# A chain of two transformer-like blocks on one core: six modulation products moved into the even attention's loop, and eight smaller reorderings

## What is computed

```python
def first_block(x, p, w_in, ...):
    h = rmsnorm(x, g_pre);  proj = h @ w_in
    (qa, ka, va, gate_a, qi, ki, wi, qb, kb, vb, fb, gate_b) = split(proj)
    att_a = dsa_branch(qa, ka, va, qi, ki, wi)     # top-k keys by an indexer
    att_b = fox_branch(qb, kb, vb, log_f)          # causal, with forgetting
    m_a, m_b = split(sigmoid(h @ w_merge))
    out = (m_a * (att_a * silu(gate_a)) @ w_branch_a
         + m_b * (att_b * silu(gate_b)) @ w_branch_b) @ w_out
    x = x + rmsnorm(out, g_post)
    return x + rmsnorm(sigmoid(x @ w_ple_gate) * (p @ w_ple), g_ple)
# second block, 2 layers, on x and a context of 256 tokens; each layer l:
#   modulation = silu(c) @ w_mod[l]  -> 6 rows of 1024: shift, scale, gate
#   even layer: differential attention (8 heads x 2 maps) and a short convolution
#   odd layer: neighbourhood attention and a Fourier mix
```

## Time and profile before

| | us |
|---|---|
| median of three runs | 1328.12 (1324.62 to 1328.36) |
| the profiled execution | 1323.46 |
| its span | 1321.5 |
| PE busy | 1246.7 (94%) |
| DVE, ACT, POOL busy | 669.7, 630.4, 456.8 |
| granted clock of TensorE, mean | 0.985 |

### The profile page before, as it was taken

How to read it: one execution, slowest core, us unless ns; L and a number is a source line. 1 busy time by engine, 2 the same in 40 slices (tenths; PEclk the granted TensorE clock), 3 DMA queues, 4 the chain that set the end, 5 groups by cost and what they waited for, 6 DMA issues and landing times.

```text
span 1321.5 us, 19566 instructions
## 1 busy us (share of the span) xinstructions
PE 1246.7 (94%) x7148; PEld 993.4 (75%) x7148; DVE 669.7 (51%) x1296; ACT 630.4 (48%) x1351; POOL 456.8 (35%) x360
## 2 busy tenths in 40 slices
PE   7999999999999699679999999999999999999998
PEld 6877776776787477578887887887868878777776
DVE  4666965755315142454838668642624701555343
ACT  7544326654523244482346666644446422655533
POOL 5543443321344333260233333331451133222341
PEclk9999999999999899899999999999999999999999
DMA  6321541111431625332141220001243142222452
GB/s 230 132 72 64 192 159 64 61 37 44 156 137 66 252 103 185 128 104 104 52 151 69 105 105 33 33 33 64 96 177 142 65 149 74 68 93 64 160 156 67
DMA packets 28429, 140.33 MB, mean 106 GB/s; under 512 B 4304, under 2 KB 5712, under 8 KB 15728
## 3 DMA queue, kind: packets, MB, share of 16 engines
q1 hardware_dynamic: 21584, 117.72, 25.3%
q10 hardware_dynamic: 6752, 21.35, 4.9%
HBM read 122.74 MB, written 6.29 MB: 98 GB/s over the span
## 4 chain that ended last, share of the span: by engine, by line
PE 70%; DVE 11%; ACT 8%; POOL 4%; DMA 4%; issue 3%; ACTq 0%; DVEq 0%; SPq 0%; POOLq 0%
PE psum L648 42%; PE psum L676 5%; PE psum L768 4%; DMA w_raw<-stream 3%; POOL w_low L1231 2%; PE psum L811 2%; DVE arena L2298 2%; PE psum L1048 2%; DVE small L2295 2%; PE psum L1216 2%; PE psum L903 2%; ACT w_high L1407 2%; PE psum L636 2%; PE psum L889 1%; PE psum L1032 1%
## 5 line engine op out<-in xcount | busy, mean ns | idle before, releaser
L1231 POOL TENSOR_TENSOR w_low<-w_raw,w_high 128x512 fp32r<-128x512 f32 x256 | 345.2, 1362 | 683.5 <-ACT w_high L1407 683.3
L1407 ACT CAST w_high<-w_raw 128x512 fp32r<-128x512 f32 x256 | 153.6, 622 | 296.5 <-PE psum L648 176.1
L648 PE MATMUL psum<-x_high,w_high 128*128 128x512 f32 x528 | 219.4, 416 | 6.6 <-POOL w_low L1231 2.4
L648 PE MATMUL psum<-x_high,w_low 128*128 128x512 f32 x528 | 207.4, 393 | 0.0
L648 PE MATMUL psum<-x_low,w_high 128*128 128x512 f32 x528 | 206.8, 392 | 0.0
L648 PEld LDWEIGHTS psum<-x_high,w_high 128*128 128x128 f32 x528 | 99.9, 189 | 37.1 <-issue 15.8
L648 PEld LDWEIGHTS psum<-x_high,w_low 128*128 128x128 f32 x528 | 99.4, 188 | 21.8
L648 PEld LDWEIGHTS psum<-x_low,w_high 128*128 128x128 f32 x528 | 99.9, 189 | 16.5 <-issue 0.7
L648 PE MATMUL psum<-w_high,x_high 128*128 128x512 f32 x224 | 89.5, 400 | 3.0 <-ACT w_high L1407 2.2
L648 PE MATMUL psum<-w_high,x_low 128*128 128x512 f32 x224 | 88.0, 393 | 0.0
L648 PE MATMUL psum<-w_low,x_high 128*128 128x512 f32 x224 | 87.8, 392 | 0.0
(11 more groups left out here) (480 smaller groups left out, 2810.8 us busy)
## 6 DMA issues: line engine op xcount, KB each, us to landing
w_raw<-stream SPq DMA_DIRECT2D x98, 1024.0 KB, 4.8
x_kept<-arena ACTq DMA_DIRECT2D x8, 512.0 KB, 4.6
arena<-x_kept ACTq DMA_DIRECT2D x8, 512.0 KB, 6.3
arena<-bias ACTq DMA_DIRECT2D x8, 512.0 KB, 3.7
q_masked<-e_q_high SPq DMA_DIRECT2D x24, 96.0 KB, 2.5
arena<-x SPq DMA_DIRECT2D x4, 512.0 KB, 5.2
arena<-x ACTq DMA_DIRECT2D x4, 512.0 KB, 6.2
arena<-ctx ACTq DMA_DIRECT2D x4, 512.0 KB, 5.0
```

The costliest lines, as they stand in the source:

```text
L648: mm = pe.matmul(o, l, r, start=(first and n == 0 and kind != "fc"), stop=(last and n == len(passes) - 1))
L1231: pool.tensor_tensor(PLACE[u][1], RAW[:, g % 2, u % 4, :], PLACE[u][0].bitcast(F32), ALU.subtract).then_inc(w_lo, 1)
L1407: act.copy(PLACE[u][0], RAW[:, g % 2, u % 4, :]).then_inc(w_hi, 1)
```

## The change

Six of the twelve products, (0,4), (0,5), (1,0), (1,1), (1,2) and (1,3), leave the hosts mb1, wo0, wo1, pg0, pg1 and eo0. Each is done in whole (`modulate_whole`) at the end of step 2, 10, 18, 26, 34 and 42 of the even loop in bank 5, and its turn (`turn_row`) two steps later where i is below 4. In the stream each of the six granules of the slim chunks is followed by two product granules. ACT copies rows and columns in the next step, DVE adds the bias once behind e_ga. Casts in the loop go by `even_units`. Beside this: PE's waits for the copies of vb and n_v come later; prep_i(0) earlier on ACT and DVE; the index loop casts two steps later; two casts of n_k and those of oo0[4..7] are placed among other work; e_ga has its two first units ahead of the gate rows, with other banks from there to n_v. The diff, cut:

```diff
+HOSTS = ("ga", "gb", "vb", "mb0")
+LATE_HOSTS = ("n_k", "ud")
+EVEN_MODS = [m for m in MODS if m not in MODS[:4] + MODS[10:]]
...
+    _j, _rest = divmod(4 * _b - UNITS[SLIM[0]][0], 4)
+    if 0 <= _j < len(EVEN_MODS):
+        GRANULES += [("m", EVEN_MODS[_j], half) for half in range(2)]
...
+        GRANULE_STEPS = 8
+        MOD_AFTER = {GRANULE_STEPS * j + 2: mod for j, mod in enumerate(EVEN_MODS)}
+        TURN_AFTER = {step + 2: mod for step, mod in MOD_AFTER.items() if mod[1] < 4}
+        def even_units(s):
+            granules_in = (s - 5) // GRANULE_STEPS + 1
+            return min(fed["e"][2 * s - 1] + ROOM, UNITS[SLIM[0]][0] + 4 * granules_in + 3)
...
-            GATED, MEANS = (0, 1, 6, 2, 3, 7), (4, 5)
+            MEANS, GATED = (3, 7), (4, 5, 0, 1, 6, 2)
...
+            def modulate_whole(layer, i, bank):
+                key = (f"mod{layer}_{i}", 0)
+                acc = open_bank(key, bank)
+                for half in range(2):
+                    g = GRANULE["m", (layer, i), half]
+                    pe.wait_ge(raw_in[g % 2], 16 * (g // 2 + 1))
+                    for j in range(4):
+                        mm = pe.matmul(acc[32 * j:32 * j + 32, :], MX[:, 4 * half + j, :], RAW[:, g % 2, j, :],
+                                       start=half == 0, stop=half == 1)
+                    if not half:
+                        mm.then_inc(sig("mod_half"), 1)
+                fills_bank(mm, key)
...
-            by_tiles("wo1", X, guest_between("wo1"))
+            by_tiles("wo1", X)
...
-                guest_between("pg1")(t)
...
                 feed("e", pieces, FEED_E[s % 4][1])
+                if s in MOD_AFTER:
+                    modulate_whole(*MOD_AFTER[s], 5)
+                if s in TURN_AFTER:
+                    turn_row(*TURN_AFTER[s], open_bank(("modT", *TURN_AFTER[s]), 5))
...
+            for _ in zip(tiles("e_ga", 0, X, C), tiles("e_ga", 1, X, C)):
+                pass
...
+            def freed_in(granule):
+                if granule[0] == "w":
+                    return split_in(4 * granule[1] + 3)
+                return min([s for s, mod in MOD_AFTER.items() if mod == granule[1]], default=len(EVEN))
...
-                if g >= granule_of(UNITS["cb_1"][-1]) and g >= 2 and GRANULES[g - 2][0] == "w":
-                    while made < len(STACK_STEPS) and STACK_STEPS[made] < split_in(4 * GRANULES[g - 2][1] + 3):
+                if g >= granule_of(UNITS["cb_1"][-1]):
+                    while made < len(STACK_STEPS) and STACK_STEPS[made] < freed_in(GRANULES[g - 2]):
...
+                if c == "qa":
+                    high(UNITS["qb"][0])
+                    prep_i(0)
...
-                if n:
-                    high(fed["i"][n - 1] + ROOM)
+                if n >= 3:
+                    high(fed["i"][n - 3] + ROOM)
...
+                if s - 1 in MOD_AFTER:
+                    guest_rows(MOD_AFTER[s - 1])
+                if s - 1 in TURN_AFTER:
+                    turned_row(TURN_AFTER[s - 1])
...
-                    high(fed["e"][2 * s - 1] + ROOM)
+                    high(even_units(s))
...
+            high(UNITS["n_k"][1])
...
+                if j:
+                    high(UNITS["oo0"][3 + j])
```

More of the change, by code:

```diff
@@ L67 @@
 SLIM = tuple(f"{part}_{j}" for j in range(4) for part in ("cb", "ub", "bb"))
-HOSTS = ("ga", "gb", "vb", "mb0", "mb1", "wo0", "wo1", "pg0", "pg1", "eo0", "n_k", "ud")
-GUEST = {host: mod for host, mod in zip(HOSTS, MODS)}
+HOSTS = ("ga", "gb", "vb", "mb0")
+LATE_HOSTS = ("n_k", "ud")
+EVEN_MODS = [m for m in MODS if m not in MODS[:4] + MODS[10:]]
+GUEST = {host: mod for host, mod in zip(HOSTS + LATE_HOSTS, MODS[:4] + MODS[10:])}
 UNITS = {}
@@ L723, in modulate, with turn_row @@
                     mm.then_inc(sig("mod_half"), 1)
+            def modulate_whole(layer, i, bank):
[10 more added lines that the diff above has]
+                fills_bank(mm, key)
+            def turn_row(layer, i, acc):
+                consumed(pe, (f"mod{layer}_{i}", 0))
+                for j in range(4):
+                    mm = pe.matmul(acc[:, 2 * j:2 * j + 2], MROW[:, i % 2, P * j:P * j + P], SEL[:, 0:2],
+                                   start=True, stop=True)
+                fills_bank(mm, ("modT", layer, i))
             def turn_due():
@@ L728, in turn_due @@
                     layer, i = due.pop()
[L729 to L734, removed]
+                    turn_row(layer, i, next_bank(("modT", layer, i)))
             def gemm(chunk, x, c=None, ready=None, midway=None, part="xc"):
@@ L743, in gemm @@
                     unit(chunk, k, x, c, part)
-                    if chunk in GUEST and k in GUEST_AT.get(chunk, (1, 5)):
+                    if chunk in GUEST and k in (1, 5):
                         modulate(*GUEST[chunk], int(k > 1))
@@ L751, in gemm, with by_tiles @@
                     due.append(GUEST[chunk])
-            def by_tiles(chunk, x, after, gives_back=True):
+            def by_tiles(chunk, x, after=None, gives_back=True):
                 units = UNITS[chunk]
@@ L896, in values_both @@
                     consumed(pe, (name, "T", 2 * d + hh, 0))
+                if (name, d) == ("b", 0):
+                    for kt in range(ST):
+                        consumed(pe, ("vb", kt))
                 key = (name, "O", d)
@@ L1171, in values_near @@
                     consumed(pe, ("n", "T", 2 * d + hh))
+                if d == 0:
+                    for i in range(ST + LT):
+                        consumed(pe, ("n_v", i))
                 if d == 1:
@@ L1462, in guest_rows, with turned_row @@
                 frees(act.copy(row, ps[:, :]), key)
+            def turned_row(mod):
+                layer, i = mod
+                key = ("modT", layer, i)
+                ps = filled(act, key)
+                frees(act.copy(MC[:, layer, 4 * i:4 * i + 4, :], ps[:, 0:8].rearrange("p (a b) -> p a b", b=2)), key)
             def prep(name, pr, q):
@@ L2197, in rope_a, with prep_i @@
                 yield
+            def prep_i(pr):
+                p = prep_of("i", pr)
+                high, out = query_place(p)
+                dve.wait_ge(sig("qm_hi"), p + 1)
+                dve.tensor_tensor(out, A_QI[:, pr, :], high.bitcast(F32), ALU.subtract).then_inc(sig("qm"), 1)
             for i in range(5):
@@ L2201, in _ @@
                     pass
+                if i == 3:
+                    prep_i(0)
                 if i == 0:
@@ L2598, in _ @@
             low_mixed([XL[:, j, :] for j in range(4)] + ctx_of(CL), [XH[:, j, :] for j in range(4)] + ctx_of(CH), values, 6)
-            modulation(1, (3,))
+            for i in range(4):
+                consumed(dve, ("modT", 1, i))
+            shifts = COLS[:, COL["bmod1"][0]:COL["bmod1"][0] + 16].unsqueeze(2).broadcast_to((P, 16, 2))
+            link(dve.tensor_tensor(MC[:, 1, :, :], MC[:, 1, :, :], shifts, ALU.add))
+            scale_up(1)
             dve.wait_ge(sig("row0"), 4)
```

98 lines of the change are left out of this document (35 added, 63 removed).

## The result

The changed kernel takes 1318.07 us (median of six runs, 1314.79 to 1319.82) where the kernel before takes 1325.25 (six runs, 1322.92 to 1328.36): ratio 0.9946, 95% interval 0.9932 to 0.996. So it is faster by 7 us, in the direction and inside the range that were given, but a third of the size: 24 us were forecast. The profiled execution took 1319.82 us, its span 1317.9, against 1323.46 and 1321.5 before.

A forecast was written before the change was run, and what follows sets the result against it. It took PE, busy 94% of the span, as the bound, along with its waits and slowed clock. Terms -42.6 + 39.6 - 6 - 15 = -24.0 gave 1299.5 us profiled, 1304 median with 4.66 added; range 1284 to 1324.

The forecast's parts named there:

- term 1: Stretch 330 to 594 us: products leaving their hosts, with PE's idles and slow clock there, save 42.6 us.
- term 2: Even loop: added products, turns, later stack copies and slow clock cost 39.6 us, bounds 15 and 55.
- term 3: Early waits, mainly ahead of and in the indexer's scores: earlier prep_i(0), later casts and vb wait save 6 us.
- term 4: Behind the loop: e_ga's bank order, fewer product halves in eo0 and eo1, and moved casts save 15 us.
- Rival A: Stretch 450 to 594: ACT, not PE, holds it; gain 20 us, total 1326, no change; chance 0.10.
- (b): Loop entry: first stack copies issued behind one more granule; first score 12.3 us later, 16.4 us in all.
- (c): Loop steps 10 to 13: later copies land behind a granule, 4.2 us for 2.5, costing 1.7 once.
- (e): Loop: half clock behind the entry stall (2.7 us) and the late product half at step 26 (0.8), 3.5 us.
- (d): Loop step 26: product's second half issued behind the last 24 copies, costing 4.6 us.
- (a): Loop: six products (12.0 us) and four turns (3.2) all count, as PE is full: 15.2 us.
- B: Loop entry: stack-copy stall hidden because the granule ahead is free sooner; about 1285 us; chance 0.14.
- C: Even loop: every product waits for its granules, at slower clock; 32 us more, 1336 us; chance 0.12.

The follow-up runs named there:

- eight: Kernel before with only the eight other places edited, all twelve products where they were: 1316.95 us, ratio 0.9951.
- moves: Changed kernel with the eight other places undone, so only the six products moved: 1322.61 us, ratio 0.9987.
- no_wo1: Kernel before with the product hosted by wo1 left out (granules, row and turn), nothing added in the loop: 1312.29 us, ratio 0.9905.
- all_three: Changed kernel with stack copies of the first two heads and behind steps 10 and 23 moved in SP's queue: 1286.95 us (0.9723), again 1288.29 us (0.9714).
- x_behind: `all_three` with the four x_kept loads issued by SP once the last weight granule has landed, not by ACT: 1283.02 us, ratio 0.9679.
- last_cast: `all_three` with oo0's last unit cast ahead of ACT's four x_kept loads, not behind them: 1290.98 us, ratio 0.9741.

## Why the prediction was right in sign and wrong in size

The sign was right by the eight small places: `eight` alone gives 0.9951 where 0.987 to 0.989 follows from the prediction's sizes, and `moves`, the subject of the change, cannot be told from no change. That the time fell into the range is no success of the sum. The forecast was 20.4 us too low for the profiled execution: 1.4 in term 1, 8.2 in term 2, 3.4 in term 3 and 7.4 in term 4.

**Term 1, the stretch 330 to 594: right.** Forecast -42.6, measured -43.8 + 2.6 = -41.2 (the shift at x2's transposes less what lay ahead of the stretch). The waits of PE went as described, but for what released the granule at wo1 (above), and the chain of ACT and DVE decides at its end, as said:

```profile
499.23 1.66 ACT L1436 CAST w_high<-w_raw 128x512 fp32r<-128x512 f32 x3 [4.35 <-DMA w_raw<-stream]
...
513.70 1.06 ACT L1473 ACTIVATE q_masked<-merge_a 128x1024 fp32r<-128x1024 f32 x1
```

The second row is the first norm of x2. From 513.70 to 549.95 are 36.25 us, where 36.3 were kept; a wait of 4.35 us for a weight granule is further up the chain. `no_wo1` shows the cause at one host. Rival A, which kept the ACT spacing, fell.

**Term 2, the loop: the entry right, the later stalls too small, +39.6 forecast, +47.8 measured.** From the starts of the 48 steps:

| stretch | measured | forecast |
|---|---|---|
| x2's transposes to step 1 | +15.0 | +16.4 |
| steps 1 to 12, two products | +6.8 | +6.7 |
| steps 12 to 14 | +7.8 | +1.7 |
| steps 14 to 26, a product and a turn | +1.3 | +1.9 |
| steps 26 to 29, a product and a turn | +11.7 | +8.2 |
| steps 29 to 47, two products, two turns | +5.2 | +4.7 |

(b) was right (the two waits, 13.0 and 2.3 us, and the first score at 648.78 where "near 645" stood). The step that failed most, by 6.1 us, is **(c), "Later copies land behind a granule just issued: 4.2 for 2.5, +1.7 once"**. Two granules stand right ahead of those copies, not one, and the copies' issue waits with them for the product at the end of step 10:

```profile
w_raw<-stream SPq DMA_DIRECT2D x2, 1024.0 KB, 7.3
b_both<-k_high SPq DMA_DIRECT2D x4, 96.0 KB, 7.5
```

These copies take 7.5 us to land, the two granules 7.3; they are issued from 698.99, 5.9 us behind the start of step 10 (693.08), where it was 1.2 before (717.86 and 716.68). PE waited 5.05 us at step 13, and step 13 then took 7.25 us where it had taken 4.67, at the slow clock. **(e), the slow clock, "0.8 for the other"** was too small too, against the sign "half clock behind the entry only": from 779 to 793 the clock is 0.76, and behind the 5.85 us at the product, step 27 took 6.31 us where it had taken 4.27, 2.0 more, and the second half of the product itself took 1.94 us, not 1.0. Behind the wait at step 13, for which (e) had nothing, it is 2.6. (d), the wait at the product behind step 26, was forecast at 4.6 and was 5.85. (a) is confirmed by `all_three`, 15.6 for 15.2.

**Term 3, the early waits: -6 forecast, -2.6 measured.** The idle of 1.7 us and one of 0.9 went; of these 2.6 us, 0.9 are lost again at 321, where the clock fell in this execution and not in that of before. The step that failed is "high() in the index loop is asked two steps later, against the two waits for ACT's L1546": they are 2.9 us in the changed kernel and with the edit undone.

**Term 4, behind the loop: -15 forecast, -7.6 measured.** To x3's transposes -5.6 of 8.2: what e_ga and eo gained met a wait of 2.08 us for DVE at x3's transposes, a norm chain that I had left out, as "each is a wait with a known cover" had it. To the last product -1.7 of 3.0. And in the tail -0.3 of 3.8: the wait of 2.18 us at oo0 is gone, and comes back at oo1 as 1.8 and 0.9. The prediction priced oo0's casts, not what is late next, which is the last weight granule beside 2 MB of loads.

The errors sum up: 1.4 + 8.2 + 3.4 + 7.4 = 20.4 us, which is the 24.0 forecast less the 3.6 measured on the profiled executions. The largest missing piece of the argument is one question: what must the issue ahead of these copies wait for. The prediction asked it at the entry, (b), and was right there, and did not at step 10.

The rivals B (no entry stall) and C (every product waits) did not come: of six products three waited, two of them for 0.6 us. The changed kernel's clock is 0.92 in the loop, where waits of 2 to 13 us stand, and that of `all_three`, with waits of at most 1.4 us, is 0.99. The page "TensorE: Matmul & The Clock Gate" of the Trainium skill has in its section "HAM oscillation" that the clock falls anew wherever short work waits for its DMA; the trace agrees for the wait of 5.85 us (eight matmuls take 1.94 us behind it) and not for those of 0.6, behind which eight take 1.07:

```profile
738.35 1.07 PE L745 MATMUL psum<-w_raw,mod_x 128*32 128x512 f32 x8 [0.60 <-DMA w_raw<-stream]
```

## What to carry to other kernels

When work moves along a stream that one in-order queue feeds, look first at what else is in that queue. Copies that were issued 25 us ahead of their use may come to stand behind a wait, and their place can be worth more than the whole change (here 17 us for one place of copies and 30 for three, against the 7 of the change). And a transfer costs more when others are under way, so late loads that nobody needs yet should wait for the one that is awaited. A wait taken away is worth only the gap to what is late next.

## What was not expected of the hardware

A granule of 1 MB landed in 4.9 us by itself (`x_behind`), in 9.1 us when issued 5.4 us behind the first of four loads of 512 KB from another engine's queue (`all_three`), and in 12.6 us when issued 2 us behind it (`last_cast`); in these two it landed 14.6 and 14.7 us after the first load's start. So being issued earlier, relative to those loads, did not let it land earlier. And a copy of 96 KB took 2.5 us with no granule ahead, 4.2 behind one and 7.5 behind two. Both fit a price of a transfer that is set by the bytes under way beside or ahead of it, more than by its own. For the copies, which stand behind the granules in the same queue, no run tells the two apart.

PE waits 1.76 us for ACT near 321 us in nearly all these executions, and what its clock does behind that wait differs. From 316 to 330 the granted clock is 0.88 in `all_three`, 0.76 in `all_three_2`, the same kernel, and 1.00 in `x_behind` and `moves`. So a wait of this length may cost a slow stretch in one execution and none in the next, and a difference of about 1 us between two profiles need not be the edit's.
